# Mixer two's retention, by pairs of heads instead of head by head

## The chip, the cores and the metric

The kernel runs on one core of a Trainium2 chip. The metric is the device time of one launch in microseconds (us), as the median of several runs. A change in time of less than about 0.3% (3.1 us here) can't be told from no change.

## The reference, cut to what matters

The program is two transformer blocks over 256 tokens of width 1024, all in float32. The change touches one part of the second block's mixer: a retention with 8 heads, key width `RET_DK` = 32, value width `RET_DV` = 64, causal by blocks of 64 tokens. Per head it computes

```python
scores = jnp.einsum('bnihd,bnjhd->bnhij', qc, kc) * decay_in
y_in = jnp.einsum('bnhij,bnjhe->bnihe', scores, vc)
# ... plus the state of the chunks before, y_x
y = (y - mu) * lax.rsqrt(var + EPS) * ret_gn_w
y_ret = jax.nn.silu(rg) * y
```

`mu` and `var` are per head and token. Beside it in the same mixer stand a projection `h @ w_in`, a depthwise convolution of 31 taps with a layer norm, and (moved into this stage by the kernel) the key projection of the memory for the cross attention that follows.

## The kernel before, in words

Activations lie transposed, features on the 128 partitions and tokens along the free axis. A projection is a row of *chunks*. One chunk is a strip of 8 weight tiles of 128x128; each tile is multiplied as high and low parts of the float32 value (`whi`, `wlo`, lines 401 to 403), so a chunk has 24 matmuls. ScalarE makes `whi` (`split_hi`, line 368) and VectorE `wlo` (`split_lo`, line 379), both three chunks ahead (`LEAD`), out of a ring of four buffers that the DMAs fill. Three PSUM banks (0 to 2) take the chunks' results in turn.

The stage of mixer two is a loop over steps q = 0 to 27, written out for each engine in an order of its own: `pe_mixb` (line 1270), `act_mixb`, `dve_mixb`. Chunks 0 to 19 are the projection; chunks 20 to 27 are the memory's keys, whose 8 tiles are plain float32 matmuls from `raw` (line 1285). In a step each engine does its part of the chunk first and then some pieces of side work. Every engine takes its instructions in order, and semaphores tie the engines together.

- VectorE's step (`dve_mixb`): read chunk q out of PSUM (lines 1541, 1553, 1562), then in steps 10 to 13 the rotary embedding of one tile of `qr` (1506 to 1509), then `dve_retention`, then `split_lo` for chunk q + 3, then a portion of the convolution's 124 taps: 5 in each of steps 4 to 19 and 11 in each of steps 20 to 23 (line 1487).
- TensorE's step (`pe_mixb`): the chunk; in step 15 the spread of the memory's norm (line 423); in steps 13 to 16 two transposes of a value tile (line 1316), which wait for VectorE's read of chunk q - 1 and for ScalarE's copy of the tile before (`rv_copied`, line 1424); from step 13 (`RET0`) on, `pe_retention(pe, q - 13)`.

`pe_retention` before, with r = q - 13: in steps r = 0 to 7 the scores of head r (lines 1350, 1351): the stationary operand is 32 partitions of keys, the moving one 32 partitions of queries, and the result goes to bank 4 or 5. In VectorE's step r the scores are multiplied by the decay into `amat` (line 1571). In TensorE's step r + 1 the values of head r follow (lines 1362, 1363): 64 columns, into partitions 0 to 63 or 64 to 127 of bank 6. In a step, the scores of head r stand ahead of the values of head r - 1. A pair of heads makes one tile of 128 features, t = 0 to 3; after its second head, ScalarE copies it (`yr`, line 1456), TensorE sums it for the mean (line 1382), VectorE centres it (1575), ScalarE squares it (1473), TensorE sums the squares (line 416), ScalarE takes the root (1462), VectorE the reciprocal (1582), TensorE spreads it (1372), and VectorE scales and gates it (1586, 1592).

At step 25 TensorE waits for the last of the convolution's taps and starts its layer norm (1326).

Mixer one, in the first block, has matmuls of the kind that the change makes: `pe_scores` (line 892) writes two heads' scores on two groups of 64 partitions into banks 4 and 5, and `pe_values` (lines 920 to 924) writes two heads' values into the column halves of bank 7, one half after the other for each part.

Of the kernel before, what the change touches and what calls it, by code (L numbers as in the profile page):

```python
# [26 lines left out]
ALU = mybir.AluOpType  # L27
# [3 lines left out]
P = 128  # L31
# [3 lines left out]
NX = 256  # L35
# [8 lines left out]
HEADS = 8  # L44
HD = 64
# [8 lines left out]
RDK = 32  # L54
# [42 lines left out]
def build(nc, io):  # L97
# [12 lines left out]
    with ctx:  # L110
# [6 lines left out]
        def place(name, shape, dt=F32, at=None):  # L117

            size = int(np.prod(shape[1:])) * 4
            size = (size + 31) // 32 * 32  # L120
            where = top[0] if at is None else at[0]
            t = nc.alloc_sbuf_tensor_at(name, shape, dt, offset=where)
            if at is None:
                top[0] += size
            else:
                at[0] += size
                assert at[0] <= nc.sbuf_usable_end, (name, at[0])
            return t
# [85 lines left out]
        qr = place("qr", [P, 4, NX], F32, at)  # L214
        v2_at = at[0]
        v2 = place("v2", [P, 2, 512], F32, at)
# [3 lines left out]
        amat = place("amat", [P, 2, 384], F32, at)  # L220
# [8 lines left out]
        decay = place("decay", [P, HEADS, 384], F32, at)  # L229
# [14 lines left out]
        part = place("part", [P, NX], F32, at)  # L244
        og = place("og", [P, KT, NX], F32, at)

        ps = [ctx.enter_context(nc.psum_tensor(f"bank{i}", [P, 512], F32)) for i in range(8)]
# [47 lines left out]
        rot_mm, rot_step, rg_done = sem("rot_mm"), sem("rot_step"), sem("rg_done")  # L295
        m_scaled, m_hi, m_lo, m_sq, m_stat, m_sd, m_inv, m_bc, m_r = (
            sem(s) for s in ("m_scaled", "m_hi", "m_lo", "m_sq", "m_stat", "m_sd", "m_inv", "m_bc", "m_r"))
        rv_tr, rv_copied = sem("rv_tr"), sem("rv_copied")
        ra_mm, ra_dec, ry_mm, ry_copied = (sem(s) for s in ("ra_mm", "ra_dec", "ry_mm", "ry_copied"))
# [1036 lines left out]

        def pe_retention(pe, r):

            if r < HEADS:
                b = RDK * (r % 4)  # L1340
                pe.wait_ge(rot_step, 9 if r < 4 else 12)
                if r == 0:
                    pe.wait_ge(norm_r, N_MIXB + 1)
                if r == 1:
                    pe.wait_ge(m_sd, 1)
                if r >= 2:
                    pe.wait_ge(ra_dec, r - 1)
                out = ps[4 + r % 2]
                qh, kh = qr[b:b + RDK, r // 4, :], qr[b:b + RDK, 2 + r // 4, :]
                nc.tensor.matmul(out[:, 0:NX], kh[:, 0:P], qh[:, :], start=True, stop=True)  # L1350
                nc.tensor.matmul(out[:, NX:NX + P], kh[:, P:NX], qh[:, P:NX], start=True, stop=True).then_inc(ra_mm, 1)
            if 1 <= r <= HEADS:
                h = r - 1
                b = HD * (h % 2)
                pe.wait_ge(ra_dec, h + 1)
                pe.wait_ge(rv_copied, h // 2 + 1)
                if h == 0:
                    pe.wait_ge(rot_step, 8)
                if h >= 2 and h % 2 == 0:
                    pe.wait_ge(ry_copied, h // 2)  # L1360
                a = amat[:, h % 2, :]
                nc.tensor.matmul(ps[6][b:b + HD, 0:NX], v2[:, 0, h * HD:(h + 1) * HD], a[:, 0:NX], start=True, stop=False)
                nc.tensor.matmul(ps[6][b:b + HD, P:NX], v2[:, 1, h * HD:(h + 1) * HD], a[:, NX:NX + P], start=False,
                                 stop=True).then_inc(ry_mm, 1)
            if r >= 6 and r % 2 == 0 and (r - 6) // 2 < 4:
                t = (r - 6) // 2
                pe.wait_ge(gn_r, t + 1)
                pe.wait_ge(gn_cen, min(t + 2, 4))
                for b, tok in enumerate(blocks(NX)):
                    for h in range(2):  # L1370
                        v = col_inv[:, 1, 2 * b + h:2 * b + h + 1].to_broadcast([P, HD])
                        mm = nc.tensor.matmul(ps[7][h * HD:(h + 1) * HD, NX + tok:NX + tok + P], v, ident[:, :],
                                              start=True, stop=True)
                mm.then_inc(gn_bc, 1)
            if r >= 3 and r % 2 == 1 and (r - 3) // 2 < 4:
                t = (r - 3) // 2
                pe.wait_ge(ry_copied, t + 1)
                if t == 0:
                    pe.wait_ge(m_r, 1)
                if t >= 2:  # L1380
                    pe.wait_ge(gn_n, t - 1)
                nc.tensor.matmul(ps[7][:, 0:NX], same[:, :], yr[:, t % 2, :], start=True, stop=True).then_inc(gn_mu, 1)
            if r >= 4 and r % 2 == 0 and (r - 4) // 2 < 4:
                t = (r - 4) // 2
                pe.wait_ge(gn_sq, t + 1)
                if t == 0:
                    pe.wait_ge(rv_copied, 4)
                if t:
                    pe.wait_ge(gn_sd, t)
                token_sums(ps[3], msq[:, t % 2, :], blocks(NX), head_cols, True, True).then_inc(gn_var, 1)  # L1390
# [59 lines left out]
        def act_retention(act, r):  # L1450
            if r >= 2 and r % 2 == 0 and (r - 2) // 2 < 4:
                t = (r - 2) // 2
                act.wait_ge(ry_mm, 2 * t + 2)
                if t >= 2:
                    act.wait_ge(gn_z, t - 1)
                nc.scalar.activation(yr[:, t % 2, :], ps[6][:, 0:NX], ACT.Copy).then_inc(ry_copied, 1)
            if r >= 5 and r % 2 == 1 and (r - 5) // 2 < 4:
                t = (r - 5) // 2
                act.wait_ge(gn_var, t + 1)
                if t:  # L1460
                    act.wait_ge(gn_r, t)
                nc.scalar.activation(col_root[:, 1, :], ps[3][:, 0:4], ACT.Sqrt, bias=epsc[:, 0:1],
                                     scale=1.0 / HD).then_inc(gn_sd, 1)
            if r >= 7 and r % 2 == 1 and (r - 7) // 2 < 4:
                t = (r - 7) // 2
                act.wait_ge(gn_z, t + 1)
                nc.scalar.activation(oz2[:, t, 0, :], zt[:, t % 2, :], ACT.Copy).then_inc(z_hi, 1)
            if r >= 3 and r % 2 == 1 and (r - 3) // 2 < 4:
                t = (r - 3) // 2
                act.wait_ge(gn_cen, t + 1)  # L1470
                if t >= 2:
                    act.wait_ge(gn_var, t - 1)
                nc.scalar.activation(msq[:, t % 2, :], yr[:, t % 2, :], ACT.Square).then_inc(gn_sq, 1)
# [88 lines left out]
                nc.vector.tensor_tensor(km[:, q - 20, :], out, memr[:, :], ALU.mult).then_inc(acc_free, 1)  # L1562

        def dve_retention(dve, r):
            if r < HEADS:
                if r == 0:
                    dve.wait_ge(decay_in, 16)
                dve.wait_ge(ra_mm, r + 1)
                if r >= 2:
                    dve.wait_ge(ry_mm, r - 1)  # L1570
                nc.vector.tensor_tensor(amat[:, r % 2, :], ps[4 + r % 2][:, 0:384], decay[:, r, :], ALU.mult).then_inc(ra_dec, 1)
            if r >= 3 and r % 2 == 1 and (r - 3) // 2 < 4:
                t = (r - 3) // 2
                dve.wait_ge(gn_mu, t + 1)
                nc.vector.scalar_tensor_tensor(yr[:, t % 2, :], ps[7][:, 0:NX], -1.0 / HD, yr[:, t % 2, :], ALU.mult,
                                               ALU.add).then_inc(gn_cen, 1)
            if r >= 5 and r % 2 == 1 and (r - 5) // 2 < 4:
                t = (r - 5) // 2
                dve.wait_ge(gn_sd, t + 1)
                if t:  # L1580
                    dve.wait_ge(gn_bc, t)
                nc.vector.reciprocal(col_inv[:, 1, :], col_root[:, 1, :]).then_inc(gn_r, 1)
            if r >= 6 and r % 2 == 0 and (r - 6) // 2 < 4:
                t = (r - 6) // 2
                dve.wait_ge(gn_bc, t + 1)
                nc.vector.scalar_tensor_tensor(yr[:, t % 2, :], yr[:, t % 2, :], vecs[:, V_GNW + t:V_GNW + t + 1],
                                               ps[7][:, NX:512], ALU.mult, ALU.mult).then_inc(gn_n, 1)
                dve.wait_ge(gn_n, t + 1)
                dve.wait_ge(rg_done, t + 1)
                if t >= 2:  # L1590
                    dve.wait_ge(z_lo, t - 1)
                nc.vector.tensor_tensor(zt[:, t % 2, :], yr[:, t % 2, :], rg[:, t, :], ALU.mult).then_inc(gn_z, 1)
            if r >= 7 and r % 2 == 1 and (r - 7) // 2 < 4:
                t = (r - 7) // 2
                dve.wait_ge(z_hi, t + 1)
                nc.vector.tensor_tensor(oz2[:, t, 1, :], zt[:, t % 2, :], oz2[:, t, 0, :], ALU.subtract).then_inc(z_lo, 1)
# [583 lines left out]
```

## Time and profile before

| | |
|---|---|
| median of 3 runs | 1021.41 us (1019.83 to 1023.31) |
| the profiled execution's own time | 1020.59 us |
| its span in the trace | 1018.8 us |
| TensorE matmul, busy | 991.9 us (97%) |
| VectorE, busy | 698.7 us (69%) |
| ScalarE, busy | 507.4 us (50%) |

The busy share of TensorE is that of the records; the matmuls of one stream overlap, so the start of the next instruction tells more of what one costs than its length does. A float32 matmul leaves two matmul records and two weight loads, which is why the timeline shows "x2" for one matmul of the program. In the timeline the number in brackets is the time that the engine was idle ahead of the instruction, and what it had waited for.

### The profile page before, as it was taken

How to read it: one execution, taken by the hardware profiler on the slowest of the kernel's cores; microseconds unless marked ns; L12 is line 12 of the kernel's file. 1: busy time of each engine (PE TensorE's matmuls, PEld its weight loads, DVE VectorE, ACT ScalarE, POOL GpSimd, SP SyncE). 2: the span in 40 equal slices, each digit the busy share in tenths (PEclk: the TensorE clock that was granted, in tenths of full speed). 3: DMA queues.
4: the chain of work that ended last, by engine and by line, in shares of the span. 5: the costliest groups of instructions: out<-in, count | busy, mean ns of one | idle time of the engine just before them, and what ended most of it. 6: DMA issues, size and time to landing. Idle time of an engine off the chain costs nothing.

```text
span 1018.8 us, 19920 instructions
## 1 busy us (share of the span) xinstructions
PE 991.9 (97%) x7365; PEld 933.4 (92%) x7365; DVE 698.7 (69%) x1267; ACT 507.4 (50%) x820; POOL 37.5 (4%) x53
## 2 busy tenths in 40 slices
PE   8999999999999999999999999899999999999996
PEld 8999999998988898999998899788899899998885
DVE  5766665555577769766676659979775488885553
ACT  6544444464455556654454466232664465444441
POOL 4600000010010000000000000000000000000000
PEclk9999999999999999999999999999999999999998
DMA  7554465437543345555565564313544245556561
GB/s 254 186 184 169 183 227 171 140 130 262 213 131 111 105 153 180 185 184 187 184 223 200 176 238 156 124 43 111 200 164 147 99 171 205 186 186 208 165 196 52
DMA packets 46028, 172.82 MB, mean 170 GB/s; under 512 B 5434, under 2 KB 6226, under 8 KB 45456
## 3 DMA queue, kind: packets, MB, share of 16 engines
q1 hardware_dynamic: 44352, 163.20, 46.0%
q0 software_dynamic: 1472, 8.76, 2.6%
q8 instruction: 40, 0.66, 0.3%
q14 instruction: 20, 0.16, 0.0%
q10 hardware_dynamic: 144, 0.03, 0.0%
HBM read 170.90 MB, written 3.77 MB: 171 GB/s over the span
## 4 chain that ended last, share of the span: by engine, by line
PE 79%; DVE 12%; DMA 3%; ACT 3%; issue 3%; SPq 0%; DVEq 0%; ACTq 0%
PE bank L401 18%; PE bank L402 18%; PE bank L403 18%; PE bank L405 11%; PE bank L406 6%; DVE cy L1487 3%; DVE wlo L379 3%; DMA raw<-in_w_mix 2%; ACT whi L368 1%; PE bank L1285 1%; DVE x L490 1%; DVE res L715 1%; PE bank L1670 1%; PE bank L892 1%; DMA res<-in_res 1%
## 5 line engine op out<-in xcount | busy, mean ns | idle before, releaser
L401 PE MATMUL bank<-x,whi 128*128 128x256 f32 (+1 forms) x1464 | 419.3, 286 | 3.7 <-DVE x L490 2.8
L402 PE MATMUL bank<-x,whi 128*128 128x256 f32 (+1 forms) x1464 | 415.1, 284 | 0.0
L403 PE MATMUL bank<-x,wlo 128*128 128x256 f32 (+1 forms) x1464 | 413.5, 282 | 0.0
L379 DVE TENSOR_TENSOR wlo<-raw,whi 128x1024 fp32r<-128x1024 f32 (+1 forms) x285 | 359.8, 1266 | 21.0 <-ACT whi L368 21.0
L368 ACT ACTIVATE whi<-raw 128x1024 fp32r<-128x1024 f32 (+1 forms) x285 | 309.0, 1087 | 113.0 <-PE bank L403 62.2
L401 PEld LDWEIGHTS bank<-x,whi 128*128 128x128 f32 x1464 | 275.4, 188 | 12.6 <-issue 5.1
L403 PEld LDWEIGHTS bank<-x,wlo 128*128 128x128 f32 x1464 | 275.9, 188 | 0.0
L402 PEld LDWEIGHTS bank<-x,whi 128*128 128x128 f32 x1464 | 275.2, 188 | 0.2
L405 PE MATMUL bank<-hid,whi 128*128 128x512 f32 x432 | 150.8, 393 | 0.0
L406 PE MATMUL bank<-hid,wlo 128*128 128x256 f32 x432 | 121.0, 280 | 0.0
L405 PEld LDWEIGHTS bank<-hid,whi 128*128 128x128 f32 x432 | 81.3, 188 | 18.6
L406 PEld LDWEIGHTS bank<-hid,wlo 128*128 128x128 f32 x432 | 80.9, 187 | 0.0
L470 ACT ACTIVATE x<-res,gains 128x256 fp32r<-128x256 f32 (+2 forms) x48 | 24.4, 514 | 84.1 <-DVE res L715 53.9
L599 ACT ACTIVATE hid<-hd 128x272 f32 (+3 forms) x44 | 18.7, 424 | 86.6 <-DVE hd L629 86.6
L712 DVE SCALAR_TENSOR_TENSOR res<-bank,res 128x256 f32<-128x256 f32 (+1 forms) x40 | 16.8, 421 | 58.6 <-PE bank L406 58.6
L401 PE MATMUL bank<-hid,whi 128*128 128x272 f32 x176 | 50.7, 288 | 0.0
L403 PE MATMUL bank<-hid,wlo 128*128 128x272 f32 x176 | 50.5, 287 | 0.0
L402 PE MATMUL bank<-hid,whi 128*128 128x272 f32 x176 | 50.5, 287 | 0.0
L1487 DVE SCALAR_TENSOR_TENSOR cy<-glu,convw,cy 128x256 f32<-128x256 f32 x120 | 49.2, 478 | 0.0
L405 PE MATMUL bank<-oz,whi 128*128 128x512 f32 x128 | 45.7, 399 | 0.8 <-DVE oz L1534 0.8
L626 DVE TENSOR_TENSOR tu<-bank,rstd 128x272 f32<-128x272 f32 (+1 forms) x44 | 19.0, 432 | 36.9 <-PE bank L403 36.9
L622 DVE TENSOR_TENSOR tg<-bank,rstd 128x272 f32<-128x272 f32 (+1 forms) x44 | 19.0, 433 | 32.1 <-PE bank L403 29.9
(281 smaller groups left out, 1208.0 us busy)
## 6 DMA issues: line engine op xcount, KB each, us to landing
raw<-in_w_f2in SPq DMA_DIRECT2D x44, 512.0 KB, 3.4
raw<-in_w_f1in SPq DMA_DIRECT2D x42, 512.0 KB, 3.4
raw<-in_w_mix SPq DMA_DIRECT2D x35, 512.0 KB, 3.8
raw<-in_w_up SPq DMA_DIRECT2D x32, 512.0 KB, 4.2
raw<-in_w_down SPq DMA_DIRECT2D x32, 512.0 KB, 4.4
raw<-in_w_f1out SPq DMA_DIRECT2D x16, 704.0 KB, 4.1
raw<-in_w_f2out SPq DMA_DIRECT2D x16, 704.0 KB, 4.2
raw<-in_w_mixb SPq DMA_DIRECT2D x20, 512.0 KB, 3.5
```

The costliest lines, as they stand in the source:

```text
L368: nc.scalar.activation(whi[:, s, 0:tiles * P], raw[:, s, 0:tiles * P], ACT.Copy).then_inc(w_hi, 1)
L379: nc.vector.tensor_tensor(wlo[:, s, 0:tiles * P], raw[:, s, 0:tiles * P], whi[:, s, 0:tiles * P], ALU.subtract).then_inc(w_lo, 1)
L401: nc.tensor.matmul(out, whi[:, s, w], hi, start=first, stop=False)
L402: nc.tensor.matmul(out, whi[:, s, w], lo, start=False, stop=False)
L403: mm = nc.tensor.matmul(out, wlo[:, s, w], hi, start=False, stop=last)
L405: nc.tensor.matmul(out, whi[:, s, w], both, start=first, stop=False)
L406: mm = nc.tensor.matmul(out[:, 0:NX], wlo[:, s, w], hi, start=False, stop=last)
L470: nc.scalar.activation(x_tile(0, m, full), res_tile(m, full), ACT.Copy, scale=gain(n, m)).then_inc(x_hi, 1)
L599: nc.scalar.activation(hid(0, u, width), hd[:, 0:width], ACT.Copy).then_inc(f["hhi"], 1)
L622: nc.vector.tensor_tensor(tg[:, 0:width], out, rstd[:, 0:width], ALU.mult).then_inc(acc_free, 1)
L626: nc.vector.tensor_tensor(tu[:, 0:width], out, rstd[:, 0:width], ALU.mult).then_inc(acc_free, 1)
L1487: nc.vector.scalar_tensor_tensor(cy[:, t, :], src, w, cy[:, t, :], ALU.mult, ALU.add).then_inc(conv_step, 1)
```

## The change

In odd steps r = 1, 3, 5, 7 the scores of two heads, 2u and 2u + 1 with u = r // 2, are issued together: first both heads' 256-column part, then both heads' 128-column part, the heads alternating between neighbouring groups of 32 partitions and between banks 4 and 5. In even steps r = 2, 4, 6, 8 the values of both heads follow in the same manner, alternating between the column halves of bank 6. VectorE multiplies both heads' scores by their decays in the odd step. The semaphores `ra_mm` and `ry_mm` count pairs, `ra_dec` still counts heads. The number and the shapes of the instructions stay as they were. The scores of heads 0, 2, 4, 6 stand one step later than before; those of heads 1, 3, 5, 7 and all that follows a pair keep their steps; the values of heads 0, 2, 4, 6 move one step back to those of their partners.

```diff
-            if r < HEADS:
-                b = RDK * (r % 4)
-                pe.wait_ge(rot_step, 9 if r < 4 else 12)
-                if r == 0:
-                    pe.wait_ge(norm_r, N_MIXB + 1)
-                if r == 1:
-                    pe.wait_ge(m_sd, 1)
-                if r >= 2:
-                    pe.wait_ge(ra_dec, r - 1)
-                out = ps[4 + r % 2]
-                qh, kh = qr[b:b + RDK, r // 4, :], qr[b:b + RDK, 2 + r // 4, :]
-                nc.tensor.matmul(out[:, 0:NX], kh[:, 0:P], qh[:, :], start=True, stop=True)
-                nc.tensor.matmul(out[:, NX:NX + P], kh[:, P:NX], qh[:, P:NX], start=True, stop=True).then_inc(ra_mm, 1)
-            if 1 <= r <= HEADS:
...
+            if r % 2 == 1 and r // 2 < HEADS // 2:
+                u = r // 2
+                pe.wait_ge(rot_step, 9 if u < 2 else 12)
+                if u == 0:
+                    pe.wait_ge(norm_r, N_MIXB + 1)
                     pe.wait_ge(m_sd, 1)
+                else:
+                    pe.wait_ge(ra_dec, 2 * u)
+                for keys, queries, lo in ((slice(0, P), slice(0, NX), 0), (slice(P, NX), slice(P, NX), NX)):
+                    for half in range(2):
+                        b = RDK * ((2 * u + half) % 4)
+                        n = queries.stop - queries.start
+                        mm = nc.tensor.matmul(ps[4 + half][:, lo:lo + n], qr[b:b + RDK, 2 + u // 2, keys],
+                                              qr[b:b + RDK, u // 2, queries], start=True, stop=True)
+                mm.then_inc(ra_mm, 1)
+            if r % 2 == 0 and 0 <= r // 2 - 1 < HEADS // 2:
+                u = r // 2 - 1
+                pe.wait_ge(ra_dec, 2 * u + 2)
+                pe.wait_ge(rv_copied, u + 1)
+                if u == 0:
                     pe.wait_ge(rot_step, 8)
+                else:
+                    pe.wait_ge(ry_copied, u)
+                for part, (queries, lo) in enumerate(((slice(0, NX), 0), (slice(P, NX), NX))):
+                    for half in range(2):
+                        b, h = HD * half, 2 * u + half
+                        n = queries.stop - queries.start
+                        mm = nc.tensor.matmul(ps[6][b:b + HD, queries], v2[:, part, h * HD:(h + 1) * HD],
+                                              amat[:, half, lo:lo + n], start=part == 0, stop=part == 1)
+                mm.then_inc(ry_mm, 1)
...
-                act.wait_ge(ry_mm, 2 * t + 2)
+                act.wait_ge(ry_mm, t + 1)
...
-            if r < HEADS:
-                if r == 0:
+            if r % 2 == 1 and r // 2 < HEADS // 2:
+                u = r // 2
+                if u == 0:
                     dve.wait_ge(decay_in, 16)
-                dve.wait_ge(ra_mm, r + 1)
-                if r >= 2:
-                    dve.wait_ge(ry_mm, r - 1)
-                nc.vector.tensor_tensor(amat[:, r % 2, :], ps[4 + r % 2][:, 0:384], decay[:, r, :], ALU.mult).then_inc(ra_dec, 1)
+                else:
+                    dve.wait_ge(ry_mm, u)
+                dve.wait_ge(ra_mm, u + 1)
+                for half in range(2):
+                    nc.vector.tensor_tensor(amat[:, half, :], ps[4 + half][:, 0:384], decay[:, 2 * u + half, :],
+                                            ALU.mult).then_inc(ra_dec, 1)
```

## Rows read from the trace of the kernel before

**Rows 1.** The page's busy times: engine, us, share of the span, instructions.

```profile
PE 991.9 (97%) x7365; PEld 933.4 (92%) x7365; DVE 698.7 (69%) x1267; ACT 507.4 (50%) x820; POOL 37.5 (4%) x53
```

**Rows 2.** Windows of mixer two: stretch, length, busy time by engine, clock, DMA share, GB/s.

```profile
610.00:668.00 58.00, 54.81 (x419) 50.77 (x418) 56.70 (x121) 28.15 (x46) 0.00 (x0) 1.00 0.39 137
668.00:684.00 16.00, 16.00 (x100) 13.30 (x99) 9.05 (x24) 5.44 (x11) 0.00 (x0) 1.00 0.11 34
684.00:706.00 22.00, 20.63 (x116) 17.04 (x114) 21.91 (x59) 3.12 (x8) 0.00 (x0) 1.00 0.33 108
```

**Rows 3.** Timeline of TensorE, step 15 to chunk 16: start, length, instruction.

```profile
654.50 0.69 PE L1350 MATMUL bank<-qr 32*128 32x256 f32 x2
655.03 0.38 PE L1351 MATMUL bank<-qr 32*128 32x128 f32 x2
655.34 0.65 PE L1362 MATMUL bank<-amat,v 128*64 128x256 f32 x2
655.82 0.38 PE L1363 MATMUL bank<-amat,v 128*64 128x128 f32 x2
656.13 0.39 PE L401 MATMUL bank<-x,whi 128*128 128x256 f32 x1
```

**Rows 4.** Timeline of TensorE, mixer one's pairs: scores, what follows, values.

```profile
279.39 0.97 PE L892 MATMUL bank<-kn,qn 64*128 64x144 f32 x8
280.29 0.39 PE L401 MATMUL bank<-x,whi 128*128 128x272 f32 x1
...
296.02 0.65 PE L920 MATMUL bank<-pts,v 128*64 128x256 f32 x4
296.50 0.39 PE L922 MATMUL bank<-pts,v 128*64 128x128 f32 x4
296.82 0.65 PE L924 MATMUL bank<-pts,vm 16*64 16x256 f32 x4
```

**Rows 5.** Timeline of TensorE: what follows chunk 16, then chunk 17's start and end.

```profile
659.08 0.38 PE L1316 MATMUL bank<-ident,tu 128*128 128x128 f32 x2
...
661.37 0.47 PE L401 MATMUL bank<-x,whi 128*128 128x256 f32 x1
...
664.48 0.69 PE L1350 MATMUL bank<-qr 32*128 32x256 f32 x2
```

**Rows 6.** Timelines of VectorE, then TensorE, in step 14 and step 15.

```profile
652.51 0.15 DVE L1512 RECIPROCAL col_inv<-col_root 128x2 f32<-128x2 f32 x1
652.59 0.54 DVE L1571 TENSOR_TENSOR amat<-bank,decay 128x384 f32<-128x384 f32 x1
653.04 1.22 DVE L379 TENSOR_TENSOR wlo<-raw,whi 128x1024 fp32r<-128x1024 f32 x1
...
652.93 0.38 PE L423 MATMUL bank<-ident,col_inv 128*128 128x128 f32 x2
654.15 0.41 PE L1316 MATMUL bank<-ident,tg 128*128 128x128 f32 x2 [0.84 <-ACT v L1424]
```

**Rows 7.** Timeline of VectorE, its waits in step 16 and in step 20.

```profile
661.76 0.42 DVE L1575 SCALAR_TENSOR_TENSOR yr<-bank,yr 128x256 f32<-128x256 f32 x1 [0.81 <-PE bank L1382]
...
680.97 0.42 DVE L1562 TENSOR_TENSOR km<-bank,memr 128x256 f32<-128x256 f32 x1 [1.18 <-PE bank L1285]
681.82 0.56 DVE L1571 TENSOR_TENSOR amat<-bank,decay 128x384 f32<-128x384 f32 x1 [0.42 <-PE bank L1351]
683.24 0.42 DVE L1575 SCALAR_TENSOR_TENSOR yr<-bank,yr 128x256 f32<-128x256 f32 x1 [0.86 <-PE bank L1382]
...
683.98 4.44 DVE L1487 SCALAR_TENSOR_TENSOR cy<-glu,convw,cy 128x256 f32<-128x256 f32 x11
```

**Rows 8.** Timeline of TensorE, step 25.

```profile
705.38 0.66 PE L1372 MATMUL bank<-ident,col_inv 128*64 128x128 f32 x8 [1.37 <-DVE col_inv L1582]
```

**Rows 9.** TensorE in mixer one: an idle stretch, and the window around it.

```profile
289.51 0.87 PE L907 MATMUL bank<-ident,att 128*128 128x128 f32 x3 [1.67 <-DVE qn L1100]
...
288.00:292.00 4.00, 2.48 (x12) 2.18 (x14) 3.53 (x8) 1.86 (x7) 0.23 (x1) 0.68 0.75 243
```

More of the change, by code:

```diff
@@ L1352, in pe_retention @@
-            if 1 <= r <= HEADS:
[L1353 to L1357, printed above, removed]
-                    pe.wait_ge(rot_step, 8)
[L1359 to L1364, printed above, removed]
+                else:
+                    pe.wait_ge(ra_dec, 2 * u)
```

## The prediction, made before the changed kernel was run

> **What bounds the kernel now.** I read the page's busy times first: TensorE is busy for 97% of the span [rows 1], so less matmul time should mean less time, wherever TensorE isn't itself waiting. That has to be read from the stage, so next came the windows over mixer two. They show three stretches [rows 2]. From 610 to 668 us VectorE is busy for 56.70 of 58 us: it leads, and TensorE, with 3.2 us idle, follows it. From 668 to 684 TensorE is busy throughout and VectorE for only 9.05 of 16 us: TensorE leads. From 684 to 706 VectorE is full again (21.91 of 22): the portions of 11 taps. So only what the change saves on TensorE's way through the middle stretch, and shortly ahead of it, can move VectorE's last portions and with them the end of the stage. The rest of TensorE's saving becomes idle time.
>
> **What one head and one pair cost.** From the timeline I take starts, not lengths. One head's scores cost 655.03 - 654.50 = 0.53 us and 655.34 - 655.03 = 0.31 us, together 0.84; its values 0.48 + 0.31 = 0.79 [rows 3]. Mixer one shows pairs. Its values for two heads, the same shapes, take 296.50 - 296.02 = 0.48 us and 296.82 - 296.50 = 0.32 us for four records each [rows 4]: two heads on column halves cost what one costs. Its scores for two heads on two groups of 64 partitions, with 272 and 144 columns, take 280.29 - 279.39 = 0.90 us [rows 4], against 0.84 for one head here with 256 and 128. So row groups overlap too. Groups of 32 partitions with another one beside them the trace doesn't show; bounds are 0.84 (full overlap) and 1.68 (none), and I take 0.84, since the 64-partition row has 416 columns against 384, and 0.84 x 416 / 384 = 0.91 us.
>
> A score matmul that comes right behind a chunk costs something ahead of itself as well. Chunk 17 takes 664.48 - 661.37 = 3.11 us up to the scores behind it; chunk 16 takes 659.08 - 656.13 = 2.95 up to the transposes behind it [rows 3, 5]: 0.16 us for the change to 32 rows. The Trainium skill's "TensorEngine Tiling (Array Packing)", section Key Properties, says that changing the tiling mode drains the engine, whereas going from one tile to another in the same mode does not. This trace agrees as to the first with its 0.16 us. Applied to each change of shape, of which there are 25 before and 16 after, the rule would give up to 1.4 us where I count 0.3 below; I leave it out of the sum, as the other changes are already within the 0.31 and 0.48 us above.
>
> **The sum, on the way that sets the end.** Total on TensorE: 4 x 0.84 + 4 x 0.79 = 6.5 us less. What of it lands:
>
> 1. *Steps 13 and 14: nothing directly.* In step 13 the scores and TensorE's wait for the rotary go; but its next transposes need VectorE's read of chunk 13, which VectorE, without a pause, reaches no sooner. The 0.84 us and the wait turn into about 1.3 us idle in step 14.
> 2. *Step 15: 0.7 us.* VectorE no longer has a decay in step 13, so its reciprocal, at 652.51 now, comes one decay sooner. One decay is 653.04 - 652.59 = 0.45 us from start to start, and the reciprocal's result is there at about 652.2. TensorE's spread waits for it instead of for its own chunk, and stands at 652.2 where it stood at 652.93 [rows 6]. Behind it the wait of 0.84 us for ScalarE's two copies stays [rows 6]. Bounds: 0, if another wait comes in, and 1.2.
> 3. *From there to the end of chunk 20: 4.1 us.* Here TensorE has now five heads' scores (2 to 6) and five heads' values (1 to 5): 5 x 0.84 + 5 x 0.79 = 8.15 us. After: two pairs of scores and three of values: 2 x 0.84 + 3 x 0.79 = 4.05. The difference is 4.1.
> 4. *Changes to 32 rows: 0.3 us.* Before, scores follow directly on chunks 17, 18 and 19; after, on chunk 18 alone. 2 x 0.16.
> 5. *Step 20: 0.4 us.* VectorE reads chunk 20 and then waits 0.42 us for scores and 0.86 us for the mean's sum, which on TensorE stands behind head 6's values [rows 7]. After, the sum stands right behind the scores and is ready before the second decay is done: 0.86 less, against 0.45 for that second decay. Bounds: -0.45 and 0.86.
>
> Together 5.5 us at the start of the 11-tap portions, at 683.98 now [rows 7]. From there VectorE has no gap, so the end of the stage moves by the same 5.5 us. TensorE still waits at step 25 for VectorE's reciprocal, 1.37 us now [rows 8], some 1.6 us after; from there on nothing is changed. The upper bound for everything is VectorE without any wait: 16 - 9.05 = 6.95 idle in the middle stretch [rows 2] and 0.81 in step 16 [rows 7], 7.8 us.
>
> *Where it could give back.* The scores of a pair come in one step, both decays behind them on VectorE, and TensorE asks for both a chunk later. Behind that wait on TensorE stand the variance sums, the spread and the next chunk. In steps 14 and 16 VectorE is late; its decays should end at about 653.0 and 660.9, while TensorE, held by the copies in the one case and by chunk 17 in the other, asks at about 653.6 and 661.8: margins of 0.6 and 0.9 us. Later they are over 2 us. I price it at nothing; with that cover gone, both waits would cost at most one decay, 0.45 us each. `wlo` for chunk 17 and on is made by VectorE in step q - 3, done over 3 us before use. The DMA queue has nothing new: each load is released by a chunk's end, as before, and moves with it.
>
> Against the profiled execution's own time: 1020.6 - 5.5 = 1015.1 us. That execution is 0.8 us under the median shown; I forecast from between the two, 1021.0, as for all cases below: 1015.5 us. The likeliest case's own range is a gain of 4.5 to 6.5.
>
> **Rivals.**
>
> - *The clock falls.* In mixer one TensorE idles for 1.67 us, and the mean granted clock of the 4 us around it is 0.68, part of them at 1.2 GHz instead of 2.4: 4 x 0.32 = 1.3 us of full-clock work lost in that window [rows 9]. The change makes new idle time: about 1.3 us in step 14, 0.6 and 0.9 in step 15, 1.6 in step 25. The present 1.37 us [rows 8] didn't bring it about, and the stretch before it is full of work. If it happens once, in step 15 or 25, I price it at 1.3 to 1.7 us, as the low clock may reach past that window: gain about 4.0, 1017.0 us.
> - *32-row groups don't overlap,* each pair of scores costing 1.68. Against it are the 64-row pairs. It takes 2 x 0.84 from term 3 and delays VectorE by 0.84 in step 20: gain about 3.0, 1018.0 us. If the values didn't overlap either, only the order would be left, about 0.6 us: 1020.4 us. Rows 4 speak plainly against that.
> - *The change doesn't do what it says because VectorE leads all the way:* then only term 2 and one wait are left, 1.0 to 1.5 us, 1019.8 us. Against it are the 6.95 us idle.
> - *Slower: alternation itself costs.* Before, four matmuls of a head lie in two positions of the array; after, every one goes to another position than the last. If each such move emptied the array as the move from a chunk does, a pair would cost two single heads and more. The gain is used up once a pair costs about 2.1 times a head; at 2.7 times (three moves of some 0.2 us for each pair, beside no overlap) the stage is some 4 us longer: 1025.0 us. Mixer one alternates in just this way at one head's price [rows 4], hence a small chance.
>
> **How the numbers follow.** Forecast 0.64; clock 0.14; row groups of 32 don't overlap 0.08; neither overlaps or VectorE leads 0.09; slower 0.05. About 0.3%, 3.1 us, is what a measurement can tell from no change. The first two cases lie beyond it (less some scatter, the runs shown spread over 3.5 us), the third on the edge, the fourth within: faster 0.75, same 0.20, slower 0.05. The range that holds 8 in 10 goes from 1013.2 (7.4 gained, near the bound) to 1018.9 us, beyond the third case.
>
> **What would show it.** Right: the pair of scores taking about 0.84 us to the next instruction, the pair of values 0.80; VectorE's reads of chunks 18 to 20 without the present long waits except at chunk 20; the first 11-tap portion at about 678.5 us; VectorE still full from there on; an idle stretch of 1.6 us in step 25; clock 1.00. Wrong: scores pairs at 1.3 us or more, a clock of 0.5 behind steps 15 or 25, a wait of TensorE for `amat` of over 0.3 us, or the 11-tap portions starting less than 4 us sooner.

## The result, and the profile after

The changed kernel took 1013.05 us (median of 4, 1012.44 to 1016.42) against 1020.62 us for the kernel before beside it (median of 4): a ratio of 0.9929, 95% interval 0.9907 to 0.9951. Measured twice more it gave 0.9933 (0.9911 to 0.9955) and 0.9949 (0.9932 to 0.9966). It is faster, by more than the 0.3% that can be told from no change: the medians beside each other differ by 7.6, 6.0 and 5.0 us. The forecast was 1015.5 us, 5.5 us gained.

The profiled execution of the first measurement took 1016.42 us and had the clock fall inside the stage of mixer two; the trace of the second measurement (1014.82 us) has no fall there, so it is the one to compare with. Here are the windows over the same three stretches as [rows 2]. They are set 1 us earlier, because the stage begins 1.23 us earlier in this trace (stretch, length, busy time by engine, clock, DMA share, GB/s):

```profile
609.00:667.00 58.00, 53.90 (x438) 50.66 (x437) 57.03 (x122) 28.41 (x47) 0.00 (x0) 1.00 0.42 137
667.00:683.00 16.00, 16.00 (x112) 13.47 (x111) 13.44 (x36) 5.07 (x9) 0.00 (x0) 1.00 0.20 66
683.00:705.00 22.00, 20.24 (x107) 17.10 (x105) 19.94 (x52) 5.77 (x13) 0.00 (x0) 1.00 0.30 96
```

In the middle one VectorE is busy for 13.44 us where it was for 9.05: its 11-tap portions start inside it now. The timeline of TensorE (start, length, instruction) has the pairs, the counterpart of [rows 3]; four matmuls of the program are one line:

```profile
656.36 0.38 PE L1316 MATMUL bank<-ident,tu 128*128 128x128 f32 x2
656.67 0.92 PE L1351 MATMUL bank<-qr 32*128 32x256 f32 x8
657.52 0.70 PE L1386 MATMUL bank<-yr,same_head 128*128 128x256 f32 x2
657.87 0.47 PE L401 MATMUL bank<-x,whi 128*128 128x256 f32 x1
...
660.99 0.87 PE L1366 MATMUL bank<-amat,v 128*64 128x256 f32 x8
661.79 0.61 PE L416 MATMUL bank<-same_head,msq 128*128 128x2 f32 x4
```

From start to start a pair of scores takes 657.52 - 656.67 = 0.85 us and a pair of values 661.79 - 660.99 = 0.80: what one head took. VectorE's timeline has the counterparts of [rows 6] and [rows 7]:

```profile
650.80 0.16 DVE L1516 RECIPROCAL col_inv<-col_root 128x2 f32<-128x2 f32 x1
650.88 1.00 DVE L1577 TENSOR_TENSOR amat<-bank,decay 128x384 f32<-128x384 f32 x2
...
659.62 0.42 DVE L1582 SCALAR_TENSOR_TENSOR yr<-bank,yr 128x256 f32<-128x256 f32 x1
...
675.01 0.42 DVE L1566 TENSOR_TENSOR km<-bank,memr 128x256 f32<-128x256 f32 x1 [1.16 <-PE bank L1285]
675.94 1.02 DVE L1577 TENSOR_TENSOR amat<-bank,decay 128x384 f32<-128x384 f32 x2 [0.51 <-PE bank L1351]
676.88 0.41 DVE L1582 SCALAR_TENSOR_TENSOR yr<-bank,yr 128x256 f32<-128x256 f32 x1
...
677.61 4.44 DVE L1491 SCALAR_TENSOR_TENSOR cy<-glu,convw,cy 128x256 f32<-128x256 f32 x11
```

The centring (L1582) waits for nothing any more in step 16, nor in step 20; the decays (L1577) stand in twos. TensorE's waits between the two ends of the stage are these. The first is that of [rows 8], in step 25; the others are in steps 14 and 15:

```profile
699.02 0.66 PE L1376 MATMUL bank<-ident,col_inv 128*64 128x128 f32 x8 [1.76 <-DVE col_inv L1589]
...
646.37 0.44 PE L1316 MATMUL bank<-ident,tu 128*128 128x128 f32 x2 [1.31 <-DVE tu L1557]
...
651.02 0.43 PE L423 MATMUL bank<-ident,col_inv 128*128 128x128 f32 x2 [0.31 <-DVE col_inv L1516]
652.29 0.41 PE L1316 MATMUL bank<-ident,tg 128*128 128x128 f32 x2 [0.84 <-ACT v L1428]
652.63 0.87 PE L1366 MATMUL bank<-amat,v 128*64 128x256 f32 x8
```

The length of the stage is read off between two instructions of TensorE that the change leaves alone: the first transposes of step 13 and the spread of the layer norm in step 27. Before:

```profile
643.03 0.44 PE L1316 MATMUL bank<-ident,tg 128*128 128x128 f32 x2 [0.33 <-DVE tg L1553]
...
717.25 0.43 PE L423 MATMUL bank<-ident,col_inv 128*128 128x128 f32 x2 [0.59 <-DVE col_inv L1515]
```

and after:

```profile
641.80 0.44 PE L1316 MATMUL bank<-ident,tg 128*128 128x128 f32 x2 [0.33 <-DVE tg L1557]
...
710.88 0.43 PE L423 MATMUL bank<-ident,col_inv 128*128 128x128 f32 x2 [0.59 <-DVE col_inv L1519]
```

That is 74.22 us before and 69.08 after, 5.14 us less. This length repeats from trace to trace far better than the whole time does (74.19 in a second trace of the kernel before), and the experiments are judged by it.

### The profile page after: what moved, and what is told of

Its sections match the earlier page's. It is cut to its first block, busy times and chain, and to the rows that moved or that the text cites. A ratio compares the mean times of both kernels' runs of the same rounds, so it can differ in the third digit from the quotient of the medians.

```text
span 1014.6 us, 19909 instructions
## 1 busy us (share of the span) xinstructions
PE 988.9 (97%) x7365; PEld 932.3 (92%) x7365; DVE 697.7 (69%) x1267; ACT 507.6 (50%) x820; POOL 37.6 (4%) x53
## 4 chain that ended last, share of the span: by engine, by line
PE 79%; DVE 12%; ACT 3%; DMA 3%; issue 3%; SPq 0%; DVEq 0%; ACTq 0%
PE bank L401 18%; PE bank L402 18%; PE bank L403 18%; PE bank L405 12%; PE bank L406 6%; DVE cy L1491 3%; DVE wlo L379 3%; DMA raw<-in_w_mix 2%; ACT whi L368 1%; PE bank L1285 1%; DVE x L490 1%; DVE res L715 1%; PE bank L1677 1%; PE bank L1654 1%; PE bank L892 1%
```

## The experiments

The columns: executions, median, ratio to the kernel before run beside it with its 95% interval, mean granted clock over the executions (the clock that TensorE was granted as a share of the full one: 1.00 is 2.4 GHz, 0.50 is 1.2 GHz), length of the stage in the trace. A passage set off as a quotation is what was expected before that run was made.

| kernel | n | us | ratio | clock | stage us |
|---|---|---|---|---|---|
| after, first measurement | 4 | 1013.05 | 0.9929 (0.9907 to 0.9951) | 0.9970 | 70.06, clock fell in it |
| after_again | 6 | 1014.50 | 0.9933 (0.9911 to 0.9955) | 0.9963 | 69.08 |
| after_third | 6 | 1014.41 | 0.9949 (0.9932 to 0.9966) | 0.9958 | 69.08 |
| before_again | 12 | 1019.92 | 1.0001 (0.9984 to 1.0017) | 0.9946 | 74.19 |
| no_row_overlap | 8 | 1017.87 | 0.9966 (0.9942 to 0.9990) | 0.9945 | 71.12 |
| no_col_overlap | 9 | 1017.03 | 0.9960 (0.9940 to 0.9979) | 0.9950 | 72.01, clock fell in it |
| no_overlap | 12 | 1019.06 | 0.9981 (0.9964 to 0.9998) | 0.9953 | 73.03 |
| head_by_head | 10 | 1014.71 | 0.9952 (0.9938 to 0.9966) | 0.9949 | 70.12, clock fell in it |
| scores_first | 10 | 1015.45 | 0.9952 (0.9935 to 0.9970) | 0.9939 | 69.07 |
| taps_moved | 6 | 1012.63 | 0.9933 (0.9911 to 0.9954) | 0.9948 | 67.27 |
| first_taps | 6 | 1013.31 | 0.9938 (0.9919 to 0.9957) | 0.9952 | 67.28 |
| before_taps | 12 | 1019.38 | 0.9991 (0.9975 to 1.0006) | 0.9952 | 73.30 |

**Taking the overlap away.** Three kernels keep the change's order and take the overlap out. In the scores:

```diff
-                        b = RDK * ((2 * u + half) % 4)
+                        b = RDK * (2 * u % 4)
```

> Both heads' scores of a pair are taken from the first head's 32 partitions, so that the two heads stand on one row group and can't overlap; the odd heads' scores are those of the even heads. Order, waits, shapes and counts stay. Theory A (row groups overlap): a pair of scores takes 1.65 us instead of 0.85, and the kernel is 2.5 to 3 us slower than the changed one. Rival (the scores' cost is the weight loads or the drain, not the columns): the pair stays near 0.9 to 1.2 us and the kernel within 1 us of the changed one.

The pair of scores takes 1.50 us and the stage is 2.04 us longer than the changed kernel's, less than the 2.5 to 3 expected. Row groups of 32 overlap. Without the overlap two heads cost 1.50 and not 1.68, since the change of shape is paid once (record by record below). In the values:

```diff
-                for part, (queries, lo) in enumerate(((slice(0, NX), 0), (slice(P, NX), NX))):
-                    for half in range(2):
-                        b, h = HD * half, 2 * u + half
+                for half in range(2):
+                    for part, (queries, lo) in enumerate(((slice(0, NX), 0), (slice(P, NX), NX))):
+                        b, h = 0, 2 * u + half
```

> Both heads' values of a pair go head by head into the lower column half of the bank, so that they can't overlap; the upper half of the bank keeps what stood there. Order of the pairs, waits and counts stay. Theory A (column halves overlap): a pair of values takes 1.6 us instead of 0.8; with 2 or 3 of the four pairs on the way that sets the end, the kernel is 2.0 to 2.6 us slower than the changed one. Rival (only the order counts): within 0.7 us of it.

The pair of values takes 1.45 us, the stage 72.01 us. The clock fell in chunk 15, as it did in the first trace of the changed kernel (70.06 us); against that one the values cost 1.95 us, a little under the 2.0 to 2.6 expected. And both together:

> Both of the two edits together: the order and the waits of the change, with no overlap in either (odd heads' scores are those of the even heads, values all in the lower half). Theory A: the stage is within 1 us of the kernel before, 0.3 to 0.8 us faster from the order alone (VectorE's reciprocal in step 15 one decay sooner, the mean's sum ahead of the values in step 20), and 5 to 5.5 us slower than the changed kernel. Rival (the clustering of the decays and the later first scores bring 2 us or more by themselves): 2 us or more faster than before.

```profile
656.70 1.57 PE L1351 MATMUL bank<-qr 32*128 32x256 f32 x8
658.20 0.48 PE L1386 MATMUL bank<-yr,same_head 128*128 128x256 f32 x1
```

This is its timeline at the place of the line at 656.67 above. The stage is 73.03 us: 3.95 us of the gain come from the overlap, less than the 5 to 5.5 expected, and 1.19 us from the order alone, more than the 0.6 us of the prediction and the 0.3 to 0.8 of the expectation. Most of the 1.19 lies between the side work of step 15 and VectorE's read of chunk 20: 677.61 - 652.01 = 25.60 us in this trace, against 26.47 before. Two heads of one shape in a row save a change of shape there even without overlap. The records show it, two for each matmul: from 656.70 on, the four of 256 columns start 0.32, 0.22, 0.21 and 0.22 us apart, the four of 128 columns 0.10 to 0.12, and the last 0.20 ahead of the sum. Only the first and the last carry the 0.1 us more, where a single head pays both. That makes 1.50 instead of 1.68 for two heads' scores and 1.45 instead of 1.58 for their values, 2 x 0.18 + 3 x 0.13 = 0.75 us on this way. The rival by which order and clustering bring most of the gain is out.

**The order inside a pair.** The first head's two matmuls ahead of the second's, in scores and values:

```diff
-                for keys, queries, lo in ((slice(0, P), slice(0, NX), 0), (slice(P, NX), slice(P, NX), NX)):
-                    for half in range(2):
+                for half in range(2):
+                    for keys, queries, lo in ((slice(0, P), slice(0, NX), 0), (slice(P, NX), slice(P, NX), NX)):
```

> In each pair the first head's two matmuls stand ahead of the second head's two, instead of alternating: positions, banks, waits and counts stay, only the order of four instructions is other. Theory A (neighbours in the order overlap only if they lie in different positions of the array): only the first head's 128-column part lies beside the second head's 256-column part, so a pair of scores takes 1.2 to 1.3 us instead of 0.85 and a pair of values the same instead of 0.80; stage 2 to 2.8 us longer than the changed kernel's 69.1 us. Rival (the engine looks ahead past the next matmul): no change.

Here my theory missed and the rival's forecast, no change, came true. The timeline of head_by_head:

```profile
655.96 0.93 PE L1351 MATMUL bank<-qr 32*128 32x256 f32 x8
656.81 0.70 PE L1386 MATMUL bank<-yr,same_head 128*128 128x256 f32 x2
```

0.85 us as before, and a stage of 70.12 us with a clock fall in chunk 15, against 70.06 with the same fall. The interleaving in the diff is not needed for the overlap; two heads in two positions overlap in either order of these four. The records say how. Asked for the 0.04 us from 655.96 on, head_by_head's timeline has two records of 256 columns in flight, where no_overlap's has one at its 656.70; the eight start in twos about 0.01 us apart, the four of 256 columns ahead of the four of 128. One head's own two records of 256 columns start 0.32 us apart, so the neighbour at 0.01 us is the other head's: its first matmul starts beside the first head's, and doesn't wait behind the first head's second one, which stands ahead of it in the program. How far TensorE can reach ahead in this way, no run here shows.

**The 7 us against the 5.** The ratio of the first measurement, 0.9929, stands for 7.2 us, 2 us more than the stage gained.

> The changed kernel once more, to separate what the change saves from what TensorE's clock gives or takes in single executions. Theory A (the saving is what the stage's timeline shows, 5.5 us with an undisturbed clock, and the rest of the measured 7 us is the number of clock falls, each 1.5 to 1.7 us): the executions sort by their mean granted clock, those at 0.998 some 1.7 us under those at 0.996 and 3.4 under those at 0.994; the median gain over the kernel before is 5 to 7.5 us. Theory B (the change saves 7 us by itself, something outside the stage included): the gain is 7 us at equal mean clocks too.

> The kernel before, once more with a trace, because its executions had a lower mean clock (0.9937 over 22) than those of the changed kernel (0.9966 over 10). Theory A (the falls of the clock come at the same places in both, by chance, and the kernel before was unlucky): mean clock here near 0.996, and at equal clock 5 us above the changed kernel. Theory C (the kernel before falls more often, because its steps 13 to 21 keep the array less busy): mean clock again 0.993 to 0.995, and its trace shows falls within or behind the stage of mixer two more often than the changed kernel's traces.

> The changed kernel a third time. Over 10 executions its mean clock was 0.9966, over 55 of the kernel before 0.9942, and 0.9939 over 10 of a variant that differs in two steps' order only. Theory A (the number of clock falls is chance, and the 7 us of the first measurement are 5 us of stage and some 2 us of luck): mean clock between 0.993 and 0.996 this time, median gain 4.5 to 6 us. Rival (the changed kernel really keeps a higher clock): 0.9965 again, and a gain of 7.

Within each kernel the executions sort by their mean clock: over all executions of this study, 0.76 us for each 0.001 (correlation -0.74). Brought to one clock of 0.998 with that slope, the kernel before stands at 1018.0 us (three sessions and before_again, 76 executions, 1017.9 to 1018.2), the changed one at 1012.9 (16 executions, 1012.5 to 1013.1): 5.1 us, give or take about 0.6 by the scatter that is left, which agrees with the stage's 5.14. So theory B is out: no gain from outside the stage is needed.

The slope is a mean over executions and not the price of one fall, and the granted clock isn't all of the scatter. The mean also holds the low clock of the last 6 to 10 us, where TensorE has little to do.

And at a granted clock of 1.00 TensorE's pace is not always the same. The second and third traces of the changed kernel have no fall ahead of the last 10 us and equal stages, yet their spans are 1013.0 and 1011.1 us. The difference is there by 235 us: the same matmul (L854) starts at 235.51 us in one and at 232.76 in the other. Some 100 us into them, 24 matmuls of 272 columns take 102.82 - 99.80 = 3.02 us and 101.94 - 98.95 = 2.99, and over the whole stretch from 20 us on the first does 1697 matmuls in 215 us, the other 1692 in 212. Such a stretch, about 1% slower at full granted clock, stands at the start of 8 of the 13 traces, of both kernels. What sets it, no run here shows.

The falls ahead of the last 10 us begin at four places in the 13 traces: at 12 us (one trace), at 242 (two), at 288 to 290 (four) and at 646 to 648 (three); four traces have none. Each begins at the end of a wait of TensorE of 1.3 to 2.1 us or up to 1.7 us behind it. The same waits stand in the traces without a fall, so the wait alone doesn't decide. Windows of the first trace of the changed kernel, one in mixer one, two in chunk 15, behind the wait in step 14, and one behind them:

```profile
242.00:243.00 1.00, 1.00 (x8) 1.00 (x7) 1.00 (x3) 1.00 (x2) 0.51 (x1) 0.59 0.06 16
...
649.00:650.00 1.00, 1.00 (x7) 1.00 (x6) 1.00 (x4) 0.00 (x0) 0.00 (x0) 0.50 0.00 0
650.00:651.00 1.00, 1.00 (x7) 1.00 (x6) 1.00 (x3) 0.00 (x0) 0.00 (x0) 0.50 0.81 242
...
652.00:653.00 1.00, 1.00 (x9) 0.75 (x7) 1.00 (x2) 0.00 (x0) 0.00 (x0) 1.00 0.07 20
```

The first trace of the kernel before had its fall in mixer one, some 47 us later than this one's [rows 9]; the second trace of each shows none before the last 10 us, where TensorE has almost nothing left to do and the clock falls in every trace. Whether the changed kernel also falls less often stays open: its mean clock came down with each measurement (0.9970, 0.9963, 0.9958), but is still above the 0.9944 of the kernel before, and above the 0.9951 beside it in the last one. The other kernels with pairs lie between 0.9939 and 0.9953, so the pairs by themselves don't raise it. In the third, theory A's 0.993 to 0.996 and its gain of 4.5 to 6 us held (5.0 us between the medians, 1019.44 and 1014.41), the rival's 0.9965 and 7 us didn't; but 16 executions don't exclude a part of it. Of theory C the number came true, a mean clock of 0.9946 in before_again, where theory A said near 0.996. Its reason is not shown: neither trace of the kernel before has a fall in the stage. So C is neither shown nor excluded.

**Filling the wait in step 14.**

```diff
+                if q in (14, 16):
+                    pe_retention(pe, q - RET0)
                 if RV < q <= RV + 4:
```

(and the later call left out in these steps.)

> In steps 14 and 16 the pair of scores stands ahead of the value tile's transposes, so that TensorE works on them while it would wait 1.3 us for VectorE's read. Theory A (step 15 is set by VectorE's reciprocal, so TensorE's earlier scores bring nothing by themselves; what can be gained is that the idle stretch, behind which the clock fell in one trace, shrinks to 0.45 us): stage 69.0 us as before with an undisturbed clock, no low clock in step 15, median 0 to 0.7 us faster than the changed kernel. Rival (the copies of the value tiles come later and TensorE waits for them in step 15): 0.3 to 0.8 us slower.

The stage is 69.07 us, the same to 0.01. TensorE waits 0.44 us in step 14 in place of 1.31, and 1.37 us for VectorE's reciprocal in place of 0.31: step 15 is set by VectorE, as term 2 had it. The clock fell in chunk 15 in 3 of the 8 traces with the 1.3 us of waiting in step 14, and in none of the 5 without, which is too few to show a link. With a median of 1015.45 us and a mean clock of 0.9939 this kernel is not better off: the 0 to 0.7 us expected of the whole time didn't come.

**Moving taps.** VectorE still waits in steps 18 to 20 of the changed kernel and then sets the end alone. The waits are about 3.1 us (from 663 to 678 us it is busy for 11.91 of 15), not the 4 us that the expectation names.

```diff
-            n = (min(q, 20) - TAP0) * TAPS_EARLY + max(q - 20, 0) * TAPS_LATE
+            n = (min(q, 17) - TAP0) * 5 + max(min(q, 20) - 17, 0) * 7 + max(q - 20, 0) * 10
```

> The convolution's taps in portions of 7 in steps 17 to 19 (now 5), 10, 10, 10 and 8 in steps 20 to 23 (now 11): 6 taps go from where VectorE sets the end to where it waits for TensorE. Theory A (from 679 us on VectorE alone sets the end, as it does in the timeline): its 4 us of waits in steps 18 to 20 shrink to under 1 us, TensorE's 1.76 us of waiting in step 25 is gone, and the stage is 1.5 to 1.7 us shorter, bounded by TensorE. Rival (the longer portions make TensorE wait for decays and reciprocals in steps 18 to 20): under 0.5 us gained.

> The two edits together: scores ahead of the transposes in steps 14 and 16, and the taps' portions of 7 and 10. Theory A: the sum of the two, 1.5 to 2 us faster than the changed kernel, 7 us faster than the kernel before at equal clock.

> The kernel before the change with the taps' portions of 7 (steps 17 to 19) and 10 (from step 20). In it TensorE is full from 655 to 704 us and waits 1.37 us at step 25. Theory A: only that wait is gained, 1.3 to 1.4 us of stage, against 1.8 on the changed kernel, since without the pairs TensorE is the next bound. Rival (VectorE's portions set the end of the stage by themselves): 2 us or more, as 6 taps take 2.4 us.

The line that decides is TensorE's in step 25, here of taps_moved, with no wait ahead of it:

```profile
698.92 0.66 PE L1376 MATMUL bank<-ident,col_inv 128*64 128x128 f32 x8
```

The stage is 67.27 us, 1.81 us shorter, and VectorE is busy for 14.01 of the 15 us from 663 us on. At one clock the kernel stands at 1010.7 us, 2.1 us under the changed one, with 6 executions and so give or take about 1.5. By the stage it beats both kernels; by the whole time it beats the kernel before, but its ratio of 0.9933 can't be told from the changed kernel's. In first_taps the earlier scores add nothing to it (67.28 us, 1011.2 us), as they added nothing alone: the 1.5 to 2 us expected came from the taps. On the kernel before, the same edit brings 0.9 us of stage, not 1.3: the wait of 1.37 us is gone, but the one for the layer norm's reciprocal in step 27 grows from 0.59 to 1.12 us. The whole time of that kernel can't be told from that of the kernel before.

```profile
717.06 0.43 PE L423 MATMUL bank<-ident,col_inv 128*128 128x128 f32 x2 [1.12 <-DVE col_inv L1515]
```

## Why the prediction was right, step by step

The terms, from the starts in the two traces, with this trace brought to that of before at the first transposes (643.03 - 641.80 = 1.23 us):

1. *Steps 13 and 14, nothing.* Right: the wait forecast at 1.3 us is there, 1.31.
2. *Step 15, 0.7.* The side work starts at 652.63 + 1.23 = 653.86, before at 654.50 [rows 3]: 0.64. VectorE's reciprocal stands at 650.80 + 1.23 = 652.03, against 652.51 [rows 6]: one decay sooner. ScalarE's 0.84 us stayed.
3. *To VectorE's read of chunk 20, terms 3 and 4 of the prediction, 4.1 + 0.3.* 675.01 - 652.63 = 22.38 us against 680.97 - 654.50 = 26.47 [rows 3, 7]: 4.09. So the pairing came as forecast, and term 4 was mis-sized: it came to nothing. Chunk 17 takes 660.99 - 657.87 = 3.12 us up to the values behind it, where it took 3.11 up to the scores. These are the last matmuls of chunks 16 and 17 before and of chunk 17 after, then the second matmuls of chunks 16 and 17 before:

```profile
658.96 0.28 PE L403 MATMUL bank<-x,wlo 128*128 128x256 f32 x1
664.27 0.28 PE L403 MATMUL bank<-x,wlo 128*128 128x256 f32 x1
...
660.77 0.28 PE L403 MATMUL bank<-x,wlo 128*128 128x256 f32 x1
...
656.36 0.28 PE L402 MATMUL bank<-x,whi 128*128 128x256 f32 x1
661.68 0.28 PE L402 MATMUL bank<-x,whi 128*128 128x256 f32 x1
```

The next instruction starts 0.12 us later where transposes follow (659.08 [rows 5]), 0.21 where scores on 32 rows follow (664.48 [rows 5]) and 0.22 where values on 64 columns follow (660.99). So either change of shape costs 0.09 to 0.10 us, not 0.16. The rest of the prediction's 0.16 lies at the start of chunk 17: 0.31 us up to its second matmul behind the mean's sum, against 0.23 in chunk 16 behind values. Before, scores stood between; now the values of steps 17 and 19 stand right behind their chunks and pay what the scores there no longer pay. The Trainium skill's "TensorEngine Tiling (Array Packing)", section Key Properties, says that changing the tiling mode drains TensorE. The traces agree in so far as a pause stands at both changes, to rows and to columns, 0.09 to 0.10 us each; I had applied it to the rows alone. The up to 1.4 us that the prediction worked out from 9 changes fewer didn't come on top: the 4.09 us leave no room for it.

4. *Step 20, 0.4.* 677.61 - 675.01 = 2.60 us against 683.98 - 680.97 = 3.01 [rows 7]: 0.41. The mean's wait is gone, the second decay is there. The 11-tap portions start at 677.61 + 1.23 = 678.84 us, forecast about 678.5.
5. *From there, nothing.* 710.88 - 677.61 = 33.27 us, and before 717.25 - 683.98 = 33.27. TensorE's wait in step 25 is 1.76 us, forecast 1.6.

Together 0.64 + 4.09 + 0.41 = 5.14 us, 5.5 forecast. The margins for the decays held: no trace of the changed kernel shows TensorE waiting for `amat`.

Of the rivals, the clock's came in part. In the first trace chunk 15 ran at 1.2 GHz after the wait in step 14, not in step 15 or 25 as priced, and cost 70.06 - 69.08 = 1.0 us, less than the 1.3 to 1.7. From 648 to 652 us the granted clock was 0.68, 0.50, 0.50 and 0.61, 1.7 us of full-clock work lost; chunk 15 up to the spread behind it took 652.62 - 648.15 = 4.47 us there, against 651.02 - 647.59 = 3.43 in the second trace, where TensorE waits for VectorE's reciprocal in that stretch anyway. It is not the rule: of three traces of the changed kernel one has it. That 32-row groups don't overlap is excluded by the pair's 0.85 us beside the 1.50 of no_row_overlap, a price of alternation by the same 0.85 us and by head_by_head, and VectorE leading all the way by the 4.09 us that landed in step 3 above.

The median of the first measurement, 1013.05 us, was 2.5 us under the forecast and 0.15 us below the lower end of the range, 1013.2. The stage is not the cause, as it gained 0.4 us less than forecast. At one clock the gain is 5.1 us; the forecast had taken its base from one execution and three times, and the scatter between kernels of a few executions each is of the size of the miss. The other two medians, 1014.50 and 1014.41, lie in the range. So the mechanism and its size were right, and the 7.6 us of the first medians were luck in part.

## What to carry to other kernels

Before you count an engine's saving, find in the windows which engine leads in each stretch: here about 6.4 us of TensorE time were saved (4 pairs, at 0.85 + 0.80 us instead of two heads at 0.84 + 0.79 each), and the stage became 5.1 us shorter. The waits that were left to VectorE showed where the next 1.8 lay: in moving its own work into them. Small matmuls that use part of the rows or columns belong together by shape and in different positions of the array; a matmul of another shape behind a full one cost 0.1 us each time. Judge a change of half a per cent by a stretch between two untouched instructions of the trace, and beside it by the whole time at equal clock.

## What the runs showed of the hardware that was not expected

Two heads' matmuls overlap even when each head's own two follow each other: 0.85 us for a pair of scores alternating or head by head, 1.50 us when both lie on one row group. A change to 64 columns behind a full matmul costs 0.10 us, like the 0.09 of one to 32 rows. Whether and where the granted clock falls changes from one execution to the next of one program: at 242 us and 648 us in the first trace of the changed kernel, and in its second and third only in the last 10 us, where TensorE has almost run out of work. And at a granted clock of 1.00, TensorE ran about 1% slower over the first 130 to 210 us of some traces than of others, enough to put the second trace 2.75 us behind the third.
